# The last mixer's value products: two heads together, alternating between the column halves of the array

## The reference, cut to what matters

```python
o_c = jnp.einsum('bghqn,bngd->bqghd', p_c, vc)
o_s = jnp.einsum('bghqm,bgqmd->bqghd', jax.nn.softmax(s_s, axis=-1), v_sel)
o_w = jnp.einsum('bghqs,bsgd->bqghd', jax.nn.softmax(..., axis=-1), vw)
return gb[..., 0, None] * o_c + gb[..., 1, None] * o_s + gb[..., 2, None] * o_w
...
return o.astype(h.dtype) @ w_out
```

## Time and profile before

| what | value |
|---|---|
| median of 3 runs | 1797.1 us (1796.06 to 1800.09) |
| the profiled execution: time, span | 1802.17 us, 1800.4 us |
| PE, VectorE, ScalarE, POOL busy | 96%, 80%, 51%, 23% of the span |
| loop over the heads in phase N | from about 1508.8 to 1574 us |

### The profile page before, as it was taken

One profiled execution on the slowest core, in us unless ns is written; L12 is line 12 of the kernel. 1 busy time (PEld: TensorE's weight loads), 2 busy tenths in 40 slices (PEclk: granted clock), 3 DMA queues, 4 the chain that ended last, 5 costly groups with the idle time before them and its releaser, 6 DMA issues. The chain is left out here.

```text
span 1800.4 us, 36286 instructions
## 1 busy us (share of the span) xinstructions
PE 1725.6 (96%) x13975; PEld 1686.8 (94%) x13975; DVE 1442.4 (80%) x1863; ACT 911.7 (51%) x1267; POOL 405.5 (23%) x647
## 2 busy tenths in 40 slices
PE   4999999999999999999999999899999998899998
PEld 3999999999999999988999998899999897699998
DVE  7777898788869878878977899869988887778555
ACT  2434367763335533456533365566444556655444
POOL 1422221012223223120122244411222121301000
PEclk9999999999999999999999999999999998999999
DMA  9998848449987788756798856235989492137550
GB/s 317 363 317 281 291 168 271 156 156 313 327 282 251 276 277 300 267 182 216 252 309 284 297 178 217 99 125 193 306 308 286 128 245 94 47 127 248 177 186 24
DMA packets 261992, 411.44 MB, mean 229 GB/s; under 512 B 21862, under 2 KB 204672, under 8 KB 261760
## 3 DMA queue, kind: packets, MB, share of 16 engines
q1 hardware_dynamic: 225368, 290.79, 48.9%
q0 software_dynamic: 36016, 119.05, 18.5%
q10 hardware_dynamic: 504, 0.18, 0.0%
HBM read 408.90 MB, written 2.63 MB: 229 GB/s over the span
## 5 line engine op out<-in xcount | busy, mean ns | idle before, releaser
L2689 DVE TENSOR_TENSOR lo<-raw,hi 128x2048 fp32r<-128x2048 f32 (+1 forms) x257 | 581.4, 2264 | 172.0 <-ACT hi L2523 171.5
L2523 ACT CAST hi<-raw 128x2048 fp32r<-128x2048 f32 (+1 forms) x266 | 498.6, 1877 | 353.4 <-PE dacc L2253 151.1
L2251 PE MATMUL up<-operand_hi,hi 128*128 128x256 f32 x1952 | 553.2, 283 | 0.6 <-DVE lo L2689 0.6
L2252 PE MATMUL up<-operand_lo,hi 128*128 128x256 f32 x1952 | 552.7, 283 | 0.0
L2253 PE MATMUL up<-operand_hi,lo 128*128 128x256 f32 x1952 | 552.5, 283 | 0.0
L2029 POOL DMA_DIRECT2D ada<-in_ada_w_dram x448 | 267.6, 618 | 816.0 <-DVE ada_acc L2729 740.7
L2251 PEld LDWEIGHTS up<-operand_hi,hi 128*128 128x128 f32 x1952 | 374.8, 192 | 1.3 <-DVE lo L2689 1.0
L2252 PEld LDWEIGHTS up<-operand_lo,hi 128*128 128x128 f32 x1952 | 374.9, 192 | 0.0
L2253 PEld LDWEIGHTS up<-operand_hi,lo 128*128 128x128 f32 x1952 | 374.9, 192 | 0.0
L2729 DVE SCALAR_TENSOR_TENSOR ada_acc<-ada,c_col,ada_acc 128x512 f32<-128x512 f32 x427 | 324.1, 759 | 22.9 <-DMA ada<-in_ada_w_dram 9.3
L2251 PE MATMUL dacc<-act_hi,hi 128*128 128x256 f32 x1056 | 300.6, 285 | 9.3 <-DVE act_lo L2903 9.3
(11 more groups left out here) (434 smaller groups left out, 2733.8 us busy)
## 6 DMA issues: line engine op xcount, KB each, us to landing
ada<-in_ada_w_dram POOLq DMA_DIRECT2D x448, 256.0 KB, 4.8
raw<-in_ffn_wg_dram SPq DMA_DIRECT2D x88, 512.0 KB, 5.1
raw<-in_ffn_wu_dram SPq DMA_DIRECT2D x88, 512.0 KB, 5.1
raw<-in_ffn_wd_dram SPq DMA_DIRECT2D x88, 512.0 KB, 5.1
raw<-in_ffn_w_up_dram SPq DMA_DIRECT2D x88, 512.0 KB, 4.5
raw<-in_ffn_w_down_dram SPq DMA_DIRECT2D x46, 512.0 KB, 4.4
raw<-in_hg_w_in_dram SPq DMA_DIRECT2D x32, 512.0 KB, 6.0
raw<-in_attn_w_qkv_dram SPq DMA_DIRECT2D x24, 512.0 KB, 7.8
```

The source lines that it names most:

```text
L2251: pe.matmul(o, stat[0], mov[0], start=start, stop=False, skip_group_check=True)
L2252: pe.matmul(o, stat[0], mov[1], start=False, stop=False, skip_group_check=True)
L2523: last = act.copy(put(slab(hi, s, SPL)), take(slab(raw, s, RAW)))
L2689: last = dve.tensor_tensor(put(slab(lo, s, SPL)), take(slab(raw, s, RAW)), put(slab(hi, s, SPL)).bitcast(F32), ALU.subtract)
```

## The change

The value products of two heads are issued together, in even laps only. First comes the product over the compressed keys, then for each branch and each block of keys the product of head f = 0 and that of head f = 1, so that successive products go to alternating column halves. One increment of `npv_pe` is made for two heads. The turned probabilities have three buffers instead of two, the third over columns 10272 to 11040 of `work`, which held the first compression weights; the copies wait for the values of the pair three heads back.

```diff
-        n_pt = [view(7424 + 768 * j, 8192 + 768 * j) for j in range(2)]
+        n_pt = [view(7424, 8192), view(8192, 8960), view(10272, 11040)]
...
-            def values(n):
-                bb, f, p, _, _ = nsa_head(n)
-                pe.wait_ge(S["npt_done"], n + 2)
+            def values(bb):
+
+                p = bb // NSA_HPG
+                pe.wait_ge(S["npt_done"], 2 * bb + 3)
+                if bb >= 2:
+                    pe.wait_ge(S["no_done"], bb - 1)
                 both = bank(dacc, 2 + bb % 2)[:, 0:SEQ]
-                if f == 0:
-                    if bb >= 2:
-                        pe.wait_ge(S["no_done"], bb - 1)
-                    r = slice(64 * (bb % 2), 64 * (bb % 2) + 64)
-                    pe.matmul(both, vc_sb[r, p * P:(p + 1) * P], c_pt[r, bb // 2 * SEQ:(bb // 2 + 1) * SEQ], start=True,
-                              stop=False, skip_group_check=True)
-                o = both[64 * f:64 * f + 64, :]
+                r = slice(64 * (bb % 2), 64 * (bb % 2) + 64)
+                pe.matmul(both, vc_sb[r, p * P:(p + 1) * P], c_pt[r, bb // 2 * SEQ:(bb // 2 + 1) * SEQ], start=True,
+                          stop=False, skip_group_check=True)
                 for br, v in enumerate((vs_sb, vw_sb)):
-                    pt = n_pt[n % 2][:, br * 3 * P:(br + 1) * 3 * P]
                     for j in range(2):
-                        c = j * SEQ + p * P + 64 * f
-                        last = pe.matmul(o[:, j * P:SEQ], v[:, c:c + 64], pt[:, j * SEQ:SEQ + j * P], start=False,
-                                         stop=(f == 1 and br == 1 and j == 1), skip_group_check=True)
+                        for f in range(2):
+                            c = j * SEQ + p * P + 64 * f
+                            pt = n_pt[(2 * bb + f) % 3][:, br * 3 * P:(br + 1) * 3 * P]
+                            last = pe.matmul(both[64 * f:64 * f + 64, j * P:SEQ], v[:, c:c + 64], pt[:, j * SEQ:SEQ + j * P],
+                                             start=False, stop=(f == 1 and br == 1 and j == 1), skip_group_check=True)
                 last.then_inc(S["npv_pe"], 1)
...
-                if n >= 3:
-                    values(n - 3)
+                if n >= 4 and n % 2 == 0:
+                    values(n // 2 - 2)
...
             def probs_back(n):
                 act.wait_ge(S["npt_pe"], n + 2)
-                if n >= 2:
-                    act.wait_ge(S["npv_pe"], n - 1)
-                act.copy(n_pt[n % 2], dacc[:, 0:768]).then_inc(S["npt_done"], 1)
+                if n >= 3:
+                    act.wait_ge(S["npv_pe"], (n - 3) // 2 + 1)
+                act.copy(n_pt[n % 3], dacc[:, 0:768]).then_inc(S["npt_done"], 1)
 
             def result(n):
                 bb = n // 2
-                act.wait_ge(S["npv_pe"], n + 1)
+                act.wait_ge(S["npv_pe"], bb + 1)
```

## The result

The changed kernel is slower: 1808.49 us median of 20 runs (1798.17 to 1815.65) against 1799.23 for before (1795.21 to 1805.01, 20 runs), ratio 1.0042, 95% interval 1.0031 to 1.0053, some 7.5 us. (The ratio is estimated from all runs; the two medians alone lie 9.3 apart.) The profiled execution of it took 1815.65 (span 1814.0), at the upper end of its runs; its loop begins 3.0 later than that of before (head 0's turn at 1511.82 against 1508.81), in code that the change does not touch. So, in what follows, the loop is compared from its own start.

What follows compares the result with a forecast made beforehand. A ring over PE, VectorE, ScalarE and POOL was taken to bound the loop, no engine full. -2.5 at full clock and +5.6 for clock falls gave +3.1, so 1800.2 us from a median of 1797.1; range 1793 to 1805.

Steps and rivals of the forecast that it cites:

- Order and ring: In the loop, turn, compressed product, V, scores and the way back to an even turn take 6.29 + V for two heads.
- V: Time of one pair's value products on PE (L1691), column halves alternating: 1.5 taken, bounds 1.44 and 2.88.
- The rule on weight loads: Weight loads overlap running matmuls only where the row group differs, never so here; by it V would be 2.88 or more.
- Waits, third buffer: ScalarE's copies and the third buffer add no stall in the loop: 0, bounds -0.1 to +0.2 a lap.
- Start of the loop: Head 5's bias stays at 1520.63, VectorE busy without a break, so head 4's turn comes at 1524.51.
- Tail: From head 14's turn to the last result copy: 7.94 instead of 8.63, gain 0.69.
- The clock: PE gaps before even turns lower the granted clock: five gaps, 3.5 full falls at 1.59 each, +5.6; ends 0 and +11.
- +3.1: Forecast change of the whole kernel: -2.5 at full clock and +5.6 for falls of the clock.
- The base: Median of the plain runs of the kernel before, 1797.1, from which 1800.2 was forecast.
- The range: The changed kernel's time was expected between 1793 and 1805.
- -2.5 + 11: Gain at full clock with the upper end for the clock: five falls, two of them twice as long.
- rival 3: Every gap costs: V = 1.7 and a fall after all five gaps in the loop, +6.9, 1804.0; chance 0.16.

Runs made afterwards that it cites:

- experiments 5 and 6: 5: next scores ahead of values, changed kernel 0.9975, kernel before 0.9961. 6: changed kernel, compressed product in odd lap, eight filler calls a gap: 0.9983 of before.
- experiment 2: Changed kernel with all products of head 0 before those of head 1, still in one lap: 1.0077 of before, 1811.9 us.
- experiment 3: Kernel before with only the third buffer added, the copy waiting for the values three heads back: 1.0005 of before.
- experiment 1, four calls: Changed kernel with four filler calls (8 records on constants) in PE's gap before each even turn: 0.9999 of before, loop 61.0.
- the trace of before: First profiled execution of the kernel before, nothing changed: 1802.17 us, loop 65.1.
- second trace of before: Kernel before profiled once more, nothing changed: 1799.50 us, loop 63.9.
- experiment 1: Changed kernel with eight filler calls (16 records on constants) in PE's gap before each even turn: 1.0001 of before, 1797.96 us, loop 61.4.
- all three traces: Three profiled executions of the changed kernel, nothing altered between them: 1815.65, 1816.87 and 1800.44 us.
- first trace: First profiled execution of the changed kernel: 1815.65 us, loop 75.4.
- third trace: Third profiled execution of the changed kernel, nothing altered: 1800.44 us, loop 68.8.
- experiment 4: Changed kernel with the compressed product over all 128 array rows instead of 64, which alters the output: 1.0013 of before, 1801.18 us, loop 65.6.
- experiment 5: Next head's scores issued ahead of values: on the changed kernel 0.9975 of before, loop 56.7; on the kernel before 0.9961; changed with three fillers a gap 0.9951.

## Why the prediction was wrong

- *Order and ring*: right. 7.77 to 7.79 was forecast at full clock, 7.75 to 7.77 measured, and experiments 5 and 6 change the ring as its terms say.
- *V*: right. 1.5 taken, 1.46 measured. Two of its thoughts were not. In the order of the change the products of the two heads that stand side by side are equally wide, so no 256-column record meets a 128-column one. And without alternation a pair takes 2.15 (experiment 2), not 2.88. The rule on weight loads in the Trainium skill ("TensorE: Matmul & The Clock Gate", Part 3), by which V would be 2.88 or more, is not borne out here: 16 records in 1.46 with the row group the same.
- *Waits, third buffer*: 0, right (experiment 3; no copy L1822 waits for L1691).
- *Start of the loop*: right in its number, by luck. From head 0's turn to head 4's 15.7 was forecast (1508.81 to 1524.51), 15.86 measured. But with the gaps filled the same stretch takes 14.58 (experiment 1, four calls). The forecast carried slow time over from the trace of before: from head 0's turn to head 5's bias it has 11.82, where the second trace of before has 10.69. And the fall behind head 2's turn, 6.8 long and not in the count, cost some 1.3. There VectorE waits for the scores of head 5, where I had it busy without a break:

```profile
1523.78 0.69 DVE L1948 SCALAR_TENSOR_TENSOR work<-work,up 128x512 f32<-128x512 f32 x1 [1.20 <-PE misc L1650]
```

- *Tail*: 7.94 at full clock was forecast, 10.3 to 10.4 measured in all three traces. With the gaps filled (experiment 1) it is 7.64 (1562.12 to 1569.76). The last gap, 3.28, came with a fall every time, some 1.0 before the turn and so within the gap.
- *The clock*: the step that failed, by its size. Its count: I had five gaps and 3.5 full falls. There are six, since the one before head 4's turn is 2.05 as well, where I took VectorE to be early enough. Four or five falls followed in each trace. Its price: I took 1.59 for every fall, from the one case in the earlier trace rows, with twice that only as an end of the range. That case began late, when the values were already running. Where the clock falls about when the turn starts, it stays low for 6.6 to 6.8, so the whole way from turn to bias runs at half speed: 10.5 to 10.9 instead of 7.77, that is 2.75 to 3.1 a fall. In the first trace the falls cost 2.75 + 3.01 + 2.98 + 1.60 in the rings, 2.7 in the tail and 1.3 at the start, 14.4 in all (75.4 against 61.0 in experiment 1 with four calls), where 5.6 was forecast. The difference of 8.8, less the 1.6 by which the loop at full clock is shorter than I had it (61.0 against 62.6), gives the 7.2 by which this loop (75.4) is longer than forecast (68.2). In the third trace (68.8) the clock cost 7.8. Over many runs the kernel lost 7.5 to before, where +3.1 was forecast.
- *The base*: 2.1 of the distance between 1800.2 and 1808.49 is that the median of before is 1799.23 over 20 runs and was 1797.1 over three.
- *The range*: its upper end was made from short falls, and -2.5 + 11 from the end named in the text would have given 1805.6 even on the first median of before. The direction that carried most of the risk was named (rival 3), but with 0.16 it was too low.

The cause is shown by experiment 1: fill the gap and the loss is gone. That the kernel takes less time with the product over all rows is shown by experiment 4's interval; how much of it is the clock's, and why stretches last 3.4 or 6.8, stays open. It also stays open why some gaps of 2.0 to 2.8 come with no fall.

## What to carry to other kernels

Before making an engine's work shorter, ask where on the ring it stands: here two orders of the same heads' work differ by 0.8% (0.9961 and 1.0042 of before), and the simple swap of scores and values, which shortens nothing, beats the overlap of two halves. Work that is gathered into one lap leaves a gap in the other. On TensorE such a gap (2.0 to 3.3 here) came with a slow clock in 14 of 18 cases, and it costs only where the others wait for what follows it: the loop of experiment 5 lost nothing that can be seen. Price a fall of the clock by the work behind the gap at half speed, not by a single past case, and when a gap can't be avoided, fill it: 1.0 of filler in a gap of 2.2 to 2.6 was enough here.

## What the runs showed of the hardware that was not expected

- Alternating the output between partitions 0:64 and 64:128 ran two float32 products side by side with different stationary and moving data and accumulation into one bank: 1.46 for 16 records, against 1.44 for 8 in one half. Even one head after the other, 16 records took 2.15, since the second half started 0.71 behind the first.
- A slow stretch lasted 3.4 or 6.6 to 6.8. Stretches shown above have PE busy for the whole of it (6.60 of 6.60, 6.80 of 6.80) and the clock at 0.50 still. The long ones began within 1.0 before and 0.6 behind an even turn, the short ones later. Two short ones stand against this as a rule: 0.4 behind head 2's turn with the compressed product over 128 rows (experiment 4), and 0.1 behind head 0's turn in the trace of before (1508.81).
- At half clock all of PE's work takes longer: turn 0.78 to 1.29, compressed 0.62 to 1.15, pair 1.46 to 2.76; a weight load of 128 columns 0.19 to 0.33 (L2253, at 1490.19 and 1491.12 of the changed kernel's trace).
- The compressed product over 128 rows of the array instead of 64 was faster, not slower: 1.21 instead of 1.40 from the turn's start to the values' (experiment 4).
